# A hybrid attention and expert layer on one core: twice the dots while tokens are placed, and new orders around two layer norms and V's last tiles

## The reference

```
h = x @ w_in                              # attention: 8 differential heads, 8 stick-breaking heads
x = LayerNorm(alpha * x + concat(A, B) @ w_out)
q = x @ w_q;  s = q . subkeys             # 8 heads, two halves of 128 keys each
top 16 of each half, then the top 16 of their 16 x 16 sums: eidx, g = softmax(top)
act = gelu(x . u_tab[eidx]) * g           # 128 picked experts of 16384 for each token
x = LayerNorm(alpha * x + sum over picks of act * v_tab[eidx])
```

## Time and profile before

| | us |
|---|---|
| median of three runs (lowest, highest) | 2586.12 (2583.93, 2589.36) |
| the profiled execution's own time | 2588.59 |
| its span in the trace | 2586.9 |
| PE / DVE / POOL / ACT busy in the span | 2322.7 / 1471.0 / 633.3 / 376.7 |

### The profile page before, as it was taken

The page is one execution under the profiler, slowest core; times in us unless marked ns, Lnnn a source line. Parts: engine busy times, 40 slices in busy tenths (PEclk is TensorE's granted clock), DMA queues, the critical chain, the costliest instruction groups (busy, mean ns, idle before and its releaser), DMA issues.

```text
span 2586.9 us, 29215 instructions
## 1 busy us (share of the span) xinstructions
PE 2322.7 (90%) x11802; PEld 1688.5 (65%) x11802; DVE 1471.0 (57%) x2342; ACT 376.7 (15%) x657; POOL 633.3 (24%) x470
## 2 busy tenths in 40 slices
PE   8999999988987958788799798499999999999993
PEld 8999999946734848777799698244444444444441
DVE  3333333353567777577687484555555555555558
ACT  3333333321102001000023130000000000000001
POOL 2000000000233444222101012334344444443331
PEclk9999999998998979999999999799999999999996
DMA  6434444365996999999988989999999999999994
GB/s 252 143 142 142 142 142 142 142 264 211 398 384 245 414 368 396 421 420 417 422 303 329 397 293 410 411 419 417 417 419 418 416 416 414 411 415 415 386 415 194
DMA packets 129924, 861.41 MB, mean 333 GB/s; under 512 B 14752, under 2 KB 14880, under 8 KB 33824
## 3 DMA queue, kind: packets, MB, share of 16 engines
q1 hardware_dynamic: 63360, 425.88, 41.7%
q0 software_dynamic: 56960, 408.97, 38.8%
q10 hardware_dynamic: 9504, 25.17, 2.5%
HBM read 833.75 MB, written 26.21 MB: 332 GB/s over the span
## 4 chain that ended last, share of the span: by engine, by line
DMA 44%; PE 32%; DVE 13%; issue 5%; POOL 4%; ACT 1%; DVEq 0%; SPq 0%; ACTq 0%; POOLq 0%
DMA scratch<-peer_v,idx_v 24%; DMA arena<-peer_u,idx_u 16%; PE bank L1254 5%; DVE scratch L1646 5%; PE bank L1096 4%; PE bank L974 4%; PE bank L975 3%; PE bank L978 3%; DMA arena<-peer_v,idx_v 3%; POOL arena L578 3%; PE bank L1237 2%; PE bank L996 2%; PE bank L992 2%; PE bank L993 2%; DMA cache<-u_tiles 2%
## 5 line engine op out<-in xcount | busy, mean ns | idle before, releaser
L1585 DVE CUSTOM_DVE_ANT_0 arena<-arena,x 128x2048 f32<-128x2048 f32 x256 | 583.4, 2287 | 239.5 <-DMA arena<-peer_u,idx_u 239.1
L578 POOL DMA_INDIRECT arena<-peer_u,idx_u x256 | 339.9, 1328 | 787.5 <-DVE dots L1585 744.5
L1646 DVE SCALAR_TENSOR_TENSOR scratch<-scratch,gate 128x2048 f32<-128x2048 f32 x112 | 263.3, 2350 | 367.8 <-DMA scratch<-peer_v,idx_v 367.4
L593 POOL DMA_INDIRECT scratch<-peer_v,idx_v x112 | 228.3, 2038 | 462.6 <-DVE scratch L1646 446.6
L1254 PE MATMUL bank<-scratch,cache 128*128 128x128 f32 x2048 | 247.6, 281 | 56.7 <-DMA cache<-u_tiles 56.5
L1254 PE MATMUL bank<-scratch,ln_rows 128*128 128x128 f32 x2048 | 244.8, 279 | 40.5 <-DMA ln_rows<-u_tiles 38.7
L1254 PEld LDWEIGHTS bank<-scratch,cache 128*128 128x128 f32 x2048 | 239.1, 196 | 63.6 <-DMA cache<-u_tiles 63.6
L1254 PEld LDWEIGHTS bank<-scratch,ln_rows 128*128 128x128 f32 x2048 | 236.3, 194 | 47.0 <-DMA ln_rows<-u_tiles 45.0
L1297 DVE TENSOR_TENSOR arena_rounded<-arena,w_high 128x1024 fp32r<-128x1024 f32 x96 | 114.3, 1228 | 266.7 <-ACT w_high L660 266.7
L1274 PE MATMUL bank<-ln_rows,scratch 128*128 128x512 f32 x512 | 232.1, 596 | 30.8 <-DVE arena L1620 30.8
L1274 PE MATMUL bank<-ln_rows,arena 128*128 128x512 f32 x512 | 230.2, 592 | 0.0
(11 more groups left out here) (210 smaller groups left out, 2845.6 us busy)
## 6 DMA issues: line engine op xcount, KB each, us to landing
ln_rows<-u_tiles SPq DMA_DIRECT2D x64, 1024.0 KB, 14.0
cache<-u_tiles SPq DMA_DIRECT2D x64, 1024.0 KB, 14.4
ln_rows<-peer_v SPq DMA_DIRECT2D x64, 1024.0 KB, 9.6
cache<-peer_v SPq DMA_DIRECT2D x64, 1024.0 KB, 9.1
arena<-w_heads SPq DMA_DIRECT2D x32, 1024.0 KB, 5.1
arena<-w_out SPq DMA_DIRECT2D x24, 1024.0 KB, 8.0
arena<-w_heads SPq DMA_DIRECT2D x8, 2048.0 KB, 8.5
arena<-w_q SPq DMA_DIRECT2D x16, 1024.0 KB, 7.3
```

Of the source, the lines that this page charges most:

```text
L578: pool.indirect_dma_start(out=u_row[k % U_SLOTS], out_offset=None, in_=peer_u, in_offset=bass.IndirectOffsetOnAxis(ap=idx_u[:, p % 2, k:k ...
L593: pool.indirect_dma_start(out=v_row[slot], out_offset=None, in_=peer_v, in_offset=bass.IndirectOffsetOnAxis(ap=idx_v[:, q % 2, k:k + 1], a ...
L1585: dve.tensor_tensor_reduce(u_row[slot], u_row[slot], x1[:, 0 if p < H else 2, :], 1.0, 0.0, ALU.mult, ALU.add, dots[:, p % 2, k:k + 1]).th ...
L1646: dve.scalar_tensor_tensor(out=residual2, in0=v_row[slot], scalar=coef[:, GROUPS_DENSE + q, k:k + 1], in1=residual2, op0=ALU.mult, op1=ALU ...
```

## The change

- While tokens are placed, DVE does a dot ahead of every eight tokens in place of every sixteen (`HOT_PER_DOT` = 8): 16 dots per block. 16 fewer are left after the last token, and the first two `gate_dense` stand ahead of these.
- ACT's `activate(8)` and `activate(9)` move to where their dots are now done: behind the store of block 0's matrix, and into block 1's placing.
- In the first layer norm of blocks 1 and 2, three dots move from behind the moments, the shift and the affine to the waits ahead of them.
- ACT copies queries and keys of step 0 ahead of `gate_numerators(0, 2)` and those of step 1 ahead of `activate(2)`.
- PE does the last four V tiles first for block 0, then for block 1 (`use_tile`), with a semaphore of its own for block 0.
- The final norm goes block 0, 2, 1, and the last five rows of block 2 (`AMONG`) stand between the steps of block 0's norm.

```diff
-HOT_PER_DOT = 16
+HOT_PER_DOT = 8
-LN2_ORDER = (2, 0, 1)
+LN2_ORDER = (0, 2, 1)
+
+AMONG = 5
...
+            queries(0)
             gate_numerators(0, 2)
-            queries(0)
+            queries(1)
             activate(2)
-            queries(1)
             activate(3)
             queries(2)
             queries(3)
...
-                if t == HOT_AT[1] + P // HOT_PER_TILE + 4:
-                    activate(H + 1)
...
-                        if b and n == 2 * HOT_PER_DOT + 7:
-                            activate(H)
+                        if b and n == 11 * HOT_PER_DOT + 3:
+                            activate(H + 1)
                         if b == 0 and n == P - 1:
                             act.wait_ge(a_copied, 2 * P // 4)
                             act.dma_start(a_kept[:, 0:LOW_KEYS, :], by_expert[0]).then_inc(a_spilled, 16)
                             act.dma_start(a_kept[:, LOW_KEYS:TILES, :], by_expert[1]).then_inc(a_spilled, 16)
+                            activate(H)
...
-            for t in range(TILES):
+            def use_tile(t, blocks):
+
                 at = TILES + t
-                pe.wait_ge(tile_loaded[at % RING], (at // RING) * 16 + 16)
+                if 0 in blocks:
+                    pe.wait_ge(tile_loaded[at % RING], (at // RING) * 16 + 16)
...
-                for b, coefs in enumerate((a_slot[:, c % A_SLOTS, t % A_CHUNK, :], own)):
+                coefs = (a_slot[:, c % A_SLOTS, t % A_CHUNK, :], own)
+                for b in blocks:
...
-                mm.then_inc(tile_used, 1)
+                if 1 in blocks:
+                    mm.then_inc(tile_used, 1)
+                elif t == TILES - 1:
+                    mm.then_inc(dense0_done, 1)
+
+            for t in range(TILES - RING):
+                use_tile(t, (0, 1))
+
+            for b in range(DENSE):
+                for t in range(TILES - RING, TILES):
+                    use_tile(t, (b,))
...
-                dve.wait_ge(tile_used, 2 * TILES)
+                if b == 0:
+                    dve.wait_ge(dense0_done, 1)
+                else:
+                    dve.wait_ge(tile_used, 2 * TILES)
...
             add_residual(1, 1, out_banks(1), 2 * 4)
-            dots_of(1, 4, 7)
+            dots_of(1, 4, 9)
             add_residual(1, 2, out_banks(2), 3 * 4)
-            dots_of(1, 7, 10)
+            dots_of(1, 9, 13)
             add_residual(1, 3, out_banks(3), 4 * 4)
             ln1_moments(1)
-            dots_of(1, 10, 12)
+            dots_of(1, 13, 14)
             ln1_shift(1)
-            dots_of(1, 12, 14)
+            dots_of(1, 14, 15)
             ln1_affine(1, 0)
             ln1_affine(1, 1)
-            dots_of(1, 14, 16)
+            dots_of(1, 15, 16)
...
-            for at in range(i, TOGETHER):
-                dot(at)
             dve.wait_ge(a_copied, 2 * DENSE * P // 4)
             for c in range(A_SLOTS):
                 gate_dense(c)
+            for at in range(i, TOGETHER):
+                dot(at)
...
-            for j in range(added, H * K):
+            for j in range(added, H * K - AMONG):
                 add_row(j)
-            for n, b in enumerate(LN2_ORDER):
-                if b < DENSE:
-                    add_dense(b)
-                ln2(n, b)
+            left = [H * K - AMONG]
+
+            def last_row():
+                if left[0] < H * K:
+                    add_row(left[0])
+                    left[0] += 1
+
+            add_dense(0)
+            last_row()
+            ln2(0, 0, last_row)
+            ln2(1, 2)
+            add_dense(1)
+            ln2(2, 1)
```

More of the change, by code:

```diff
@@ L310, in build @@
             sem, ("picks_turned", "picks_copied", "hot_ready", "hot_used", "a_copied", "a_spilled", "tile_used"))
-        residual2_ready, dense_added = sem("residual2_ready"), sem("dense_added")
+        residual2_ready, dense_added, dense0_done = sem("residual2_ready"), sem("dense_added"), sem("dense0_done")
         wo_used, out_projected, residual_ready, stats_ready = map(
@@ L1263, in _ @@
             pe.wait_ge(a_copied, 2 * DENSE * P // 4)
-            for t in range(TILES):
+            def use_tile(t, blocks):
                 at = TILES + t
-                pe.wait_ge(tile_loaded[at % RING], (at // RING) * 16 + 16)
+                if 0 in blocks:
+                    pe.wait_ge(tile_loaded[at % RING], (at // RING) * 16 + 16)
                 c = t // A_CHUNK
-                if t % A_CHUNK == 0:
+                if t % A_CHUNK == 0 and 0 in blocks:
                     pe.wait_ge(a_loaded[c % A_SLOTS], (c // A_SLOTS) * 16 + 16)
@@ L1271, in _ @@
                 own = by_expert[0][:, t, :] if t < LOW_KEYS else by_expert[1][:, t - LOW_KEYS, :]
-                for b, coefs in enumerate((a_slot[:, c % A_SLOTS, t % A_CHUNK, :], own)):
+                coefs = (a_slot[:, c % A_SLOTS, t % A_CHUNK, :], own)
+                for b in blocks:
                     for j in range(4):
-                        mm = pe.matmul(bank[4 * b + j][:, :], coefs, tile[at % RING][:, j * 512:(j + 1) * 512],
+                        mm = pe.matmul(bank[4 * b + j][:, :], coefs[b], tile[at % RING][:, j * 512:(j + 1) * 512],
                                        start=(t == 0), stop=(t == TILES - 1), skip_group_check=True)
-                mm.then_inc(tile_used, 1)
+                if 1 in blocks:
[7 more added lines that the diff above has]
+                    use_tile(t, (b,))
         @block.vector
@@ L1655, in add_dense, with ln2 @@
                        .then_inc(dense_added, 1)
-            def ln2(n, b):
+            def ln2(n, b, between=lambda: None):
                 rows = last_rows[b]
@@ L1665, in ln2 @@
                     dve.bn_stats(stats[:, b, j, :], rows[:, j * 512:(j + 1) * 512]).then_inc(ln2_stats, 1)
+                between()
                 dve.wait_ge(ln2_stats, 4 * (n + 1))
@@ L1681, in ln2 @@
                        .then_inc(y_ready, 1)
+                    if q % 2:
+                        between()
             dots_and_choice(0, 0, 1)
@@ L1731, in _ @@
             weigh(PLACES - 1)
-            for j in range(added, H * K):
+            for j in range(added, H * K - AMONG):
                 add_row(j)
-            for n, b in enumerate(LN2_ORDER):
-                if b < DENSE:
-                    add_dense(b)
-                ln2(n, b)
+            left = [H * K - AMONG]
[9 more added lines that the diff above has]
+            ln2(2, 1)
+            assert left[0] == H * K
 def kernel(x_prompt, x_sample, cache_diff_k, cache_diff_v, cache_sb_k, cache_sb_v, w_in, w_out, lam_q1, lam_k1,
```

## The result

The changed kernel takes 2555.26 us (median of four runs, 2551.95 to 2557.82) against 2586.28 before; the ratio is 0.9876, with an interval of 0.9863 to 0.9889. That is 31 us less. The forecast was 2549 with a range of 2535 to 2565. The execution profiled took 2557.82 us (span 2556.1), so it is compared with the one of before, span 2586.9: -30.8.

The account below looks back on a forecast made before the run. The prediction saw transfers crowded into some stages, with a PE bubble behind one; -6.6 + 7.8 + 1 - 38.1 + 0 - 1.3 = -37.2 gave 2551.4 us on the profiled execution, 2549 as median forecast, range 2535 to 2565.

Parts of the forecast that it names:

- First layer norm: Blocks 1 and 2: three dots leave DVE's chain to the next choice, -6.6 us; PE's later wait grows to some 30.
- Placing: Placing tokens of both blocks: DVE sets the pace at 5.83 us per eight tokens, +3.9 us per block.
- the slower rival: Placing: dots are not hidden, a step takes 7.56 us, +18, 2604 us; chance 0.04.
- Last token to V's start: Behind the last token: ten dots left and early gates let V start after 76.4 us, -38.1 us.
- late V tile: V's start: PE waits for the first V tile or a_kept's first chunk, up to 8 us, 2557 us; chance 0.1.
- late gate: Before V: gates wait for their gelu chunks, PE's gap stays at 30.75 us, 2578 us; hardly any gain, chance 0.03.
- V stage: From V's start: same products and gathers, transfers fill the engines, so 0 change, bound 7.5 us either side.
- The sum: Whole kernel: the stages' terms add up to -37.2 us, forecast 2549 us.
- last rows that end later against V's start: End of kernel, sign of being wrong: last rows end later against V's start than the 886.7 us before.
- The transfers decide: Rival, whole kernel: the DMA engines' bytes set the time, -33.4 us, 2553 us; chance 0.2.
- The end: Last rows and norms: DVE keeps its work, rows cover block 0's two waits for ACT, -1.3 us.

Follow-up runs that it names:

- the dots alone: Kernel before, with one dot per 8 tokens in place of 16 and the two activate calls moved, gates still behind the ten left-over dots: 2558.42 us, ratio 0.9904.
- the end alone: Kernel before, with only the changed order of the last V tiles and final norms, and rows among the norm's steps: 2585.62 us, ratio 0.9993.
- the gates alone: Kernel before, with only the two gate products moved ahead of the 26 left-over dots: 2590.57 us, ratio 1.0014.
- the norm alone: Kernel before, with only the first layer norm's new split of dots and ACT's order around the query products: 2581.06 us, ratio 0.9984.
- the gates last: Changed kernel, with the two gate products put back behind the ten left-over dots: 2553.81 us, ratio 0.9866.
- the first hole filled: Changed kernel, with ACT loading gelu chunks 2 and 3 earlier and POOL's first peer_v and one more peer_u gather issued earlier: 2552.21 us, ratio 0.9862.

## Why the prediction was right, and where it was wrong

The time lay in the range, 6 us above the forecast, but the largest term had the wrong reason, and that the sum came so near is in part luck.

- **First layer norm.** The chain gained what was worked out: affine 810.18 to 805.75, choice 825.23 to 818.59, -6.6. PE's later wait grew as foretold, 28.57 to 34.22 (some 30 forecast). At the first tile with tokens the gain was 8.6, but the profile of before is a late one there: without the norm's edit that tile starts at 1311.99 (the dots alone), 1313.58 (the end alone), 1314.62 (the gates alone) and 1316.76 (before), with it at 1307.45 (the norm alone) and 1308.14. So the 2 us beyond the forecast are no more than executions differ.
- **Placing.** 5.83 us per eight tokens was the forecast, and 93.32 / 16 = 5.83 is what block 0 took, DVE busy 93.32 of 93.32. Block 0 came out cheaper than +3.9 because its stretch before was dearer than the 89.38 that the step was taken from (91.72, at a granted clock of 0.97 for 1.00). Its first U tile alone took 6.27 us there and 3.74 after (above). A dot is hidden, then, but for DVE's own time; the 7.56 us per step of the slower rival did not occur.
- **Last token to V's start.** 76.4 us forecast, 77.52 measured. PE waits 0.69 us, for ACT's last gelu, so neither a late V tile nor a late gate took the gap's place. The size was right; that this time is what the kernel gains was wrong. With the gates alone V started 28.7 us earlier, and nothing was gained.
- **V stage: "Same products, same gathers ... 0, with 7.5 us as the bound".** This is the step that failed. The sum fixes the last rows' distance from V's start (874.4 us). But the rows follow the transfers. Their distance was 903 us with the gates alone, and 883.4 with the whole change. The prediction had named this as a sign of being wrong, last rows that end later against V's start; for the last row itself it is 905.8 for 886.7 us, 10 of them block 0's norm. That the change came near its forecast all the same is luck: sixteen dots moved happen to be worth about as much by bytes (16 x 1.05 MB / 0.42 = 39.9) as they shorten PE's way to V (37.0).
- **The transfers decide**, with 0.2, was the mechanism by the runs; that its 2553 is also the nearer number says little, as the two forecasts lie closer together than a measurement can tell. It too placed one loss wrongly: the engines did not idle once the ten gathers were in, because V's first tiles filled the ring (419 GB/s up to V's start). They idled behind V's start, while DVE waited for a gelu chunk that ACT loads late and POOL for the last gelu store; the run that loosened these came out about 3 us lower, of 4.4 us worked out, which is within the noise. The Trainium skill (DMA: Bandwidth & Descriptors, section Issuing engines are not separate DMA queues) states that transfers end up on the same sixteen engines and interleave there, whichever engine issued them. The trace agrees: with the gates alone, SP's tiles and POOL's gathers ran together at 421 GB/s ahead of V's start. As these runs read, then, an earlier transfer gains only the idle time into which it falls; where there was hardly any, the last row ended at 2549.6 with PE's gap at 7.85 us and at 2549.74 with it at 30.75.
- **The end.** -1.3 forecast, -2.1 in the trace, not to be told apart from nothing in the times (0.9993).

What stays open is the rest of the 9.0 us. It is no accident of the profile of before: from V's start to the 123rd row the norm alone gave 875.3 and the end alone 874.8 us, for 874.4. Over the same stretch it is 883.4 and 880.8 us in two executions of the changed kernel, 881.3 with the gates last, 879.2 with the first hole filled, but 874.5 in the one profiled execution with the dots alone, which has that hole too, and whose other runs took 3 to 11 us longer. Executions of one program differ by some us in the rate of this stage; more than the hole of 4.4 us, the runs do not assign.

## What to carry to other kernels

Before a gap on the busiest engine is booked as a gain, look at what the transfers do in that gap and behind it: where they are full in both, and the last result waits for them, closing the gap only reorders them, as it did here. Then an edit is priced by a table of stages, (full rate minus rate) times length before and after, and the places to look for more are the rows with the lowest rate on the way to the end, not the idle time of the engines.

## Not expected of the hardware

A gather's issue on POOL does not have one length. Of the 202 issues in the V stage of the changed kernel, the 88 during which DVE does nothing take 0.93 to 0.96 us, and the 38 during which DVE works throughout take 1.90 to 3.03. Two of them: the one at 1643.84 falls into a dot and a gate product on DVE, the one at 1666.17 into the idle time after the third DVE row below, which lasts until the fourth:

```profile
1643.84 2.74 POOL L595 DMA_INDIRECT scratch<-peer_v,idx_v  x1 [6.44 <-DVE scratch L1660]
...
1666.17 0.94 POOL L595 DMA_INDIRECT scratch<-peer_v,idx_v  x1 [4.24 <-DVE scratch L1660]
```

```profile
1643.49 2.28 DVE L1599 CUSTOM_DVE_ANT_0 arena<-arena,x 128x2048 f32<-128x2048 f32 x1
...
1645.70 0.69 DVE L1634 TENSOR_TENSOR arena<-arena,scratch 128x512 f32<-128x512 f32 x1
...
1663.55 2.35 DVE L1660 SCALAR_TENSOR_TENSOR scratch<-scratch,gate 128x2048 f32<-128x2048 f32 x1 [2.97 <-DMA scratch<-peer_v,idx_v]
1672.81 2.35 DVE L1660 SCALAR_TENSOR_TENSOR scratch<-scratch,gate 128x2048 f32<-128x2048 f32 x1 [6.91 <-DMA scratch<-peer_v,idx_v]
```

The prediction took 1.0 us from the earlier trace rows. While block 0 is placed DVE works throughout too, on one-hots and dots, and there the first twelve of sixteen issues take 0.99 to 1.01 us and the last four 2.97 to 3.48:

```profile
1374.39 1.00 POOL L580 DMA_INDIRECT arena<-peer_u,idx_u  x1 [4.83 <-DVE dots L1599]
1386.06 3.48 POOL L580 DMA_INDIRECT arena<-peer_u,idx_u  x1 [2.36 <-DVE dots L1599]
```

No dot in that stretch had to wait for it. So a busy DVE is not enough to make an issue long, and what does is not shown by these runs.
